# Prompt attention in pairs of key/value heads: one block, plain transposes, the scaling on GpSimd

## What is computed

```
ck = compress_blocks(kv[:, :, :2], cmp_w)
p_c = masked_softmax(jnp.einsum('bqhgd,bnhd->bqhgn', qg, ck[:, :, 0]), mask_c)
o_cmp = jnp.einsum('bqhgn,bnhd->bqhgd', p_c, ck[:, :, 1])
...
o = g[..., 0:1] * o_cmp + g[..., 1:2] * o_slc + g[..., 2:3] * o_win
```

## Time and profile before

| | us |
|---|---|
| median of 3 runs | 2150.6 |
| lowest, highest | 2147.47, 2154.2 |
| profiled execution, first to last instruction (its span) | 2151.5 |
| busy: TensorE | 1927.7 (90%) |
| busy: VectorE | 1031.1 (48%) |
| busy: ScalarE | 669.4 (31%) |
| busy: GpSimd | 240.4 (11%) |

### The profile page before, as it was taken

The page is one execution under the profiler, slowest core; times in us unless marked ns, Lnnn a source line. Parts: engine busy times, 40 slices in busy tenths (PEclk is TensorE's granted clock), DMA queues, the critical chain, the costliest instruction groups (busy, mean ns, idle before and its releaser), DMA issues. The chain is left out here.

```text
span 2151.5 us, 31716 instructions
## 1 busy us (share of the span) xinstructions
PE 1927.7 (90%) x13190; PEld 1745.7 (81%) x13190; DVE 1031.1 (48%) x1718; ACT 669.4 (31%) x1288; POOL 240.4 (11%) x388
## 2 busy tenths in 40 slices
PE   6997998896999999996998969788779699999996
PEld 6996666595999999986798958555478699999995
DVE  5563753235666662226463233336652566665223
ACT  2642442224333332115353220111121533333112
POOL 0010000000222220000100010123000122221000
PEclk9996999798999999998999977668789899999998
DMA  4201620011222222213112230100221222222221
GB/s 170 69 32 46 218 83 2 21 60 59 89 79 83 85 77 81 81 35 101 60 60 79 79 121 1 44 1 0 89 81 37 88 79 86 82 80 83 81 76 58
DMA packets 50321, 152.42 MB, mean 71 GB/s; under 512 B 7282, under 2 KB 16946, under 8 KB 49410
## 3 DMA queue, kind: packets, MB, share of 16 engines
q1 hardware_dynamic: 50178, 150.40, 21.6%
HBM read 138.12 MB, written 16.39 MB: 72 GB/s over the span
## 5 line engine op out<-in xcount | busy, mean ns | idle before, releaser
L686 PE MATMUL ps<-x_high,w_high 128*128 128x288 f32 x2288 | 689.8, 301 | 73.9 <-DVE x_low L708 72.6
L687 PE MATMUL ps<-x_low,w_high 128*128 128x288 f32 x2288 | 681.9, 298 | 0.0
L688 PE MATMUL ps<-x_high,w_low 128*128 128x288 f32 x2288 | 679.5, 297 | 0.0
L686 PEld LDWEIGHTS ps<-x_high,w_high 128*128 128x128 f32 x2288 | 435.6, 190 | 81.7 <-issue 51.0
L665 DVE TENSOR_TENSOR w_low<-w_raw,w_high 128x1024 fp32r<-128x1024 f32 (+1 forms) x215 | 253.5, 1182 | 441.0 <-ACT w_high L660 440.9
L688 PEld LDWEIGHTS ps<-x_high,w_low 128*128 128x128 f32 x2288 | 437.6, 191 | 0.0
L687 PEld LDWEIGHTS ps<-x_low,w_high 128*128 128x128 f32 x2288 | 436.6, 191 | 0.3
L660 ACT ACTIVATE w_high<-w_raw 128x1024 fp32r<-128x1024 f32 (+1 forms) x215 | 221.4, 1032 | 529.6 <-PE ps L688 458.9
L686 PE MATMUL ps<-g_high,w_high 128*128 128x288 f32 x704 | 211.1, 300 | 1.7 <-ACT ub L771 1.7
L687 PE MATMUL ps<-g_low,w_high 128*128 128x288 f32 x704 | 207.7, 295 | 0.0
L688 PE MATMUL ps<-g_high,w_low 128*128 128x288 f32 x704 | 206.9, 294 | 0.0
(11 more groups left out here) (399 smaller groups left out, 2485.6 us busy)
## 6 DMA issues: line engine op xcount, KB each, us to landing
w_raw<-in_w_up SPq DMA_DIRECT2D x88, 512.0 KB, 3.6
w_raw<-in_w_odd SPq DMA_DIRECT2D x36, 512.0 KB, 3.3
w_raw<-in_w_down SPq DMA_DIRECT2D x32, 512.0 KB, 3.6
w_raw<-in_w_even SPq DMA_DIRECT2D x19, 512.0 KB, 3.4
ptok<-in_cache_tok SPq DMA_DIRECT2D x32, 192.0 KB, 2.4
w_raw<-in_w_down SPq DMA_DIRECT2D x16, 384.0 KB, 3.1
w_raw<-in_w_mix SPq DMA_DIRECT2D x16, 384.0 KB, 3.1
w_raw<-in_w_mix SPq DMA_DIRECT2D x8, 512.0 KB, 3.6
```

The costliest lines, as they stand in the source:

```text
L686: pe.matmul(out, self.high[:, s, k, :], high(k0 + k)[:, cols], start=first, stop=False)
L687: pe.matmul(out, self.high[:, s, k, :], low(k0 + k)[:, cols], start=False, stop=False)
L688: mm = pe.matmul(out, self.low[:, s, k, :], high(k0 + k)[:, cols], start=False, stop=last)
```

## The change

Both blocks become one. The loop runs over 32 pairs: the two groups `h` of the same tile, branch and head together. A pair's scores go to two neighbouring PSUM banks, its weighing alternates between the groups product by product. VectorE masks and takes the negated maximum of both groups in one instruction each. It multiplies the reciprocals of the two sums by the gates, and GpSimd scales the probabilities with them in place (`spread`). The turn is then a plain transpose with the identity. ScalarE copies the turned probabilities of group 0, VectorE those of group 1. In step i TensorE takes the scores of pair i, the weighing of pair i-3 and the turn of pair i-2. The compressed branch's scores alternate between the groups; after VectorE has centred them, the rest of that branch runs between the first pairs, with the two multiplications of its probabilities on GpSimd, and its products with the values close each query tile's sums instead of opening them. SyncE's list is the same, in the one block. In the cut diff a line of "..." stands for what is left out.

```diff
+    pairs = [(qt, br, j) for qt in range(4) for br in range(2) for j in range(4)]
+    N = len(pairs)
+    SLOTS = 3
+    S, TURNED, OUT = (0, 2), (4, 5), (6, 7)
...
-            with nc.Block() as block:
...
-        S, TURNED, OUT = (0, 1, 2), (3, 4), (6, 7)
...
+        probs, pT = sb("probs", [P, SLOTS, 2, 512]), sb("pT", [P, 2, 2, 512])
+        nmx, sums = sb("nmx", [P, SLOTS, 2]), sb("sums", [P, SLOTS, 2])
...
+        def keys(p):
+
+            return P * (pairs[p][0] + 1)
...
-                def turn(u):
-
-                    pe.wait_ge(diag_done, u + 1)
-                    if u >= 2:
-                        pe.wait_ge(turned_in, u - 1)
-                    for k in range(units[u][0] + 1):
-                        mm = pe.matmul(net.ps[:, TURNED[u % 2], P * k:P * k + P], probs[:, u % 3, P * k:P * k + P], diag[:, u % 3, :], start=True, stop=True)
-                    mm.then_inc(turned, 1)
...
+                def scores(p):
+
+                    qt, br, j = pairs[p]
+                    if p >= 2:
+                        pe.wait_ge(exped, 2 * (p - 1))
+                    for h in range(2):
+                        mm = pe.matmul(net.ps[:, S[p % 2] + h, 0:keys(p)], qT[64 * h:64 * h + 64, j, P * qt:P * qt + P],
+                                       kT[64 * h:64 * h + 64, br, 0:keys(p)], start=True, stop=True)
+                    mm.then_inc(scored, 1)
+
+                def turn(p):
+
+                    for h in range(2):
+                        pe.wait_ge(normed, 2 * p + h + 1)
+                        if p == 0:
+                            pe.wait_ge(c_taken, h + 1)
+                        else:
+                            pe.wait_ge((kept0, kept1)[h], p)
+                        for k in range(pairs[p][0] + 1):
+                            mm = pe.transpose(net.ps[:, TURNED[h], P * k:P * k + P], probs[:, p % SLOTS, h, P * k:P * k + P], net.ident[:])
+                        mm.then_inc(turned, 1)
+
+                def weigh(p):
+
+                    qt, br, j = pairs[p]
+                    bank, first = OUT[qt % 2], p % 8 == 0
+                    if first and qt >= 2:
+                        pe.wait_ge(out_kept, qt - 1)
+                    if p == 8:
+                        pe.wait_ge(c_kept, 2)
+                    pe.wait_ge(kept0, p + 1)
+                    pe.wait_ge(kept1, p + 1)
                     for k in range(qt + 1):
-                        mm = pe.matmul(net.ps[64 * h:64 * h + 64, bank, P * j:P * j + P], kv[:, k, v0:v0 + 64], pT[:, u % 2, P * k:P * k + P],
-                                       start=False, stop=(br == 1 and k == qt), skip_group_check=True)
-                    mm.then_inc(summed, 1)
-
-                for i in range(N + 4):
+                        for h in range(2):
+                            v0 = (384 if br == 0 else 640) + 64 * h
+                            mm = pe.matmul(net.ps[64 * h:64 * h + 64, bank, P * j:P * j + P], kv[:, k, v0:v0 + 64], pT[:, p % 2, h, P * k:P * k + P],
+                                           start=(first and k == 0), stop=False, skip_group_check=True)
+                    mm.then_inc(weigh_done, 1)
+                    if p % 8 == 7:
+                        pe.wait_ge(c_kept, 2)
+                        for jj in range(4):
+                            for h in range(2):
+                                mm = pe.matmul(net.ps[64 * h:64 * h + 64, bank, P * jj:P * jj + P], cvd[:, h, jj, :], pTc[:, h, qt, :],
+                                               start=False, stop=(jj == 3), skip_group_check=True)
+                        mm.then_inc(weighed, 1)
+
+                for tt in range(4):
...
+                pe.wait_ge(kept, 1)
+                for qt in range(4):
+                    for j in range(4):
+                        for h in range(2):
+                            mm = pe.matmul(net.ps[:, 4 + h, P * qt + 32 * j:P * qt + 32 * j + 32],
+                                           qT[64 * h:64 * h + 64, j, P * qt:P * qt + P], ckT[64 * h:64 * h + 64, :], start=True, stop=True)
+                mm.then_inc(c_scored, 1)
+                for i in range(N + 3):
                     if i < N:
                         scores(i)
+                    if i >= 3:
+                        weigh(i - 3)
                     if 2 <= i < N + 2:
                         turn(i - 2)
-                    if i >= 4:
-                        weigh(i - 4)
+                    if i in (4, 5):
+                        h = i - 4
+                        pe.wait_ge(c_probs, h + 1)
+                        if h:
+                            pe.wait_ge(c_kept, 1)
+                        for qt in range(4):
+                            mm = pe.transpose(net.ps[:, 7, P * qt:P * qt + P], sc[:, h, qt].rearrange("p j n -> p (j n)"), net.ident[:])
+                        mm.then_inc(c_turned, 1)
...
             @block.scalar
             def _(act):
+                def keep(p):
+
+                    act.wait_ge(turned, 2 * p + 1)
+                    if p >= 2:
+                        act.wait_ge(weigh_done, p - 1)
+                    act.activation(pT[:, p % 2, 0, 0:keys(p)], net.ps[:, TURNED[0], 0:keys(p)], ACT.Copy).then_inc(kept0, 1)
+
+                for h in range(2):
+                    act.wait_ge(c_centred, h + 1)
+                    act.activation(sc[:, h], sc[:, h], ACT.Exp).then_inc(c_exped, 1)
                 for i in range(N + 5):
...
                     if i < N:
...
-                            act.wait_ge(turned, i - 2)
-                        act.activation(probs[:, i % 3, 0:n], net.ps[:, S[i % 3], 0:n], ACT.Exp, bias=nmx[:, i % 3:i % 3 + 1],
...
+                        if i >= SLOTS:
+                            act.wait_ge(turned, 2 * (i - SLOTS) + 2)
+                        for h in range(2):
+                            act.activation(probs[:, s, h, 0:keys(i)], net.ps[:, S[i % 2] + h, 0:keys(i)], ACT.Exp, bias=nmx[:, s, h:h + 1],
+                                           accum_out=sums[:, s, h:h + 1]).then_inc(exped, 1)
+                    if 1 <= i < N + 1:
+                        keep(i - 1)
+                    if i in (3, 4):
+                        act.wait_ge(c_turned, i - 2)
+                        act.activation(pTc[:, i - 3], split_free(net.bank(7), t=4, n=P), ACT.Copy).then_inc(c_kept, 1)
+                    if i >= 11 and i % 8 == 3:
+                        qt = i // 8 - 1
+                        act.wait_ge(weighed, qt + 1)
...
+            @block.gpsimd
+            def _(pool):
+                def spread(p):
+
+                    n, s = keys(p), p % SLOTS
+                    pool.wait_ge(shares, p + 1)
+                    for h in range(2):
+                        pool.tensor_scalar(probs[:, s, h, 0:n], probs[:, s, h, 0:n], sums[:, s, h:h + 1], 1.0, ALU.mult, ALU.mult).then_inc(normed, 1)
+
+                keep = split_free(c["cmp_01"], t=4, n=32)[:, :, None, :].broadcast_to([P, 4, 4, 32])
+                for h in range(2):
+                    s16 = sc[:, h].rearrange("p t j n -> p (t j) n")
+                    spread(h)
+                    pool.wait_ge(c_scaled, h + 1)
+                    pool.tensor_tensor(sc[:, h], sc[:, h], keep, ALU.mult).then_inc(c_order, 1)
+                    pool.wait_ge(c_order, h + 1)
+                    pool.tensor_tensor(s16, s16, sm[:, h].rearrange("p t j -> p (t j)")[:, :, None].broadcast_to([P, 16, 32]), ALU.mult).then_inc(c_probs, 1)
+                for p in range(2, N):
+                    spread(p)
 
...
-                for i in range(N + 2):
...
-                        r = sums[:, u % 3:u % 3 + 1]
-                        dve.wait_ge(exped, u + 1)
-                        if u >= 3:
-                            dve.wait_ge(turned, u - 2)
...
+                def centre(h):
+
+                    s16 = sc[:, h].rearrange("p t j n -> p (t j) n")
+                    m16 = mx[:, 16 * h:16 * h + 16]
+                    link(dve.tensor_reduce(m16, s16, AX, ALU.max))
+                    dve.tensor_tensor(s16, s16, m16[:, :, None].broadcast_to([P, 16, 32]), ALU.subtract).then_inc(c_centred, 1)
+
+                def share(h):
+
+                    s16, r16 = sc[:, h].rearrange("p t j n -> p (t j) n"), sm[:, h].rearrange("p t j -> p (t j)")
+                    dve.wait_ge(c_exped, h + 1)
+                    link(dve.tensor_reduce(r16, s16, AX, ALU.add))
+                    link(dve.reciprocal(r16, r16))
+                    dve.tensor_tensor(sm[:, h], sm[:, h], g5[:, 0:4, h, :, 0], ALU.mult).then_inc(c_scaled, 1)
+
+                dve.wait_ge(blocks, 1)
+                dve.tensor_copy(ckT[:], net.ps[:, 7, 0:32])
...
+                dve.wait_ge(c_scored, 1)
+                for h in range(2):
+                    dve.tensor_tensor(sc[:, h], split_free(net.bank(4 + h), t=4, j=4, n=32), neg, ALU.add).then_inc(c_taken, 1)
+                dve.wait_ge(c_taken, 2)
+                for h in range(2):
+                    centre(h)
```

(27 more changed lines are left out.)

124 lines of the change are left out of this document (20 added, 104 removed).

## The result

The changed kernel took 2072.9 to 2095.2 us in four runs, median 2084.2, beside 2147.5 to 2154.2 (median 2152.2) of the kernel before: ratio 0.965, 95% interval 0.959 to 0.972. The prediction was 2084, range 2066 to 2106. The profiled execution took 2086.2 us, its span is 2084.5 (before: 2151.5), so between the two profiles lie 67.0 us.

The account below looks back on a forecast made before the run. TensorE bounds the loop, a chain of dependent steps the compressed block. Pairs 74.6, filling 5.5, branch products 3.4, clock 4.3 and end 7.0 sum to 94.8 against 149.4 us; with 12.1 in front, 66.7 gained: 2084 us, range 2066 to 2106.

Parts of the forecast that it names:

- Heads side by side: Loop on TensorE: full overlap, so a pair's scores and weighing each cost what one head's cost; 3.16 us at four blocks.
- The rival's price: Not side by side: scores and weighing in series, 2124 us; one of the two alone, 2102 or 2105; chance 0.07.
- Plain transposes: Turn on TensorE: a transpose has one pass, not two, so a pair's turn is eight passes at 512 keys.
- VectorE, GpSimd, ScalarE hidden: Long pairs: VectorE 2.82 us, GpSimd scaling 1.4 and ScalarE about 2.1, under TensorE's 3.16.
- the rule at its worst: VectorE and GpSimd blocking in SBUF, one 0.69 us wait per pair: 2106 us; part of the GpSimd rival, chance 0.03.
- Front: Compressed block before the loop: alternating scores 6.7 us instead of 13.0, first mask at 187.2, 12.1 us gained.
- Filling and end: Loop's start and finish: 5.5 us for filling with the compressed branch's work, 7.0 for the last pair beyond its slot.
- Clock: Loop's start: first ten pairs at 1.2 GHz, costing 4.3 us; sample attention starts with a warm TensorE as today.
- The rival of the low clock: TensorE stays at 1.2 GHz: 2130 us; 2091 if it rises after pair 16, 2106 after 24; 16 or more cold, chance 0.07.
- Loads: SyncE's loads for the sample attention: last issue at 234 us, hidden before the sample attention starts near 282.

Follow-up runs that it names:

- the scores apart: Changed kernel with an earlier pair's weighing placed between the scores of the two heads; median 2133.7 us, ratio 0.9842 to the kernel before.
- the turn by products: Changed kernel with the turn as an fp32 product with the identity instead of a transpose; median 2097.3 us, ratio 0.9713 to the kernel before.
- the earlier start: Changed kernel, scores of pairs 0 and 1 ahead of the compressed scores: 2081.2 us, 0.963; second version, compressed scores split over more banks: 2076.4 us, 0.9616.
- the woven kernel before: Kernel before with only the compressed scores alternating between the two heads; median 2163.2 us, ratio 0.9996 to the kernel before.

## Why the prediction was right, point by point

**Heads side by side: right.** Full overlap was taken, and four score passes in 1.13 us and sixteen weighing passes in 1.09 show it, at 3.10 us a pair for the predicted 3.16 (2.45 for 2.52, 1.93 for 2.02). The rival's price was mis-sized in both of its halves: one alone was to add 18 to 21 us. The weighing head after head adds 5.8, since some of its passes still overlap; the scores apart add some 42 at equal mean clock, since the later scores also make the weighing wait for VectorE.

**Plain transposes: right.** Eight passes in 1.09 us; taking them back costs 18.2 us.

**VectorE, GpSimd, ScalarE hidden: right.** GpSimd's 0.69 at 512 elements came from the row of the same operation and is what it takes (1.36 for two). Doubling GpSimd's work costs 4.9 us and not 28, so the slack that the prediction described was there. What the prediction called the rule at its worst, 2106, did not come. VectorE's products with two inputs in SBUF were held up at the loop's start: the 128x16 one took 1.17 us beside a GpSimd product, where the other of its kind took 0.18, and one of the 128x2 kind 0.96 instead of 0.16; both end within 0.05 us of the GpSimd product that was running. This agrees with the Trainium skill, "SBUF — State Buffer" (Who interferes with whom). In the steady loop the product comes when GpSimd is idle, as was argued, and takes 0.16; in all, some 2 us.

**Front: right.** 12.3 us earlier to the first mask (block's start taken as zero) for the predicted 12.1, and the 7.04 us of the compressed scores for 6.7.

**Filling and end: both off, in opposite directions.** From the first mask to pair 8, 18.2 us are eight pairs at the 1.97 us that pairs 6 and 7 took at the low clock, and 2.4: the filling was 2.4, not 5.5, probably because the branch's work on VectorE and GpSimd mostly lay beside the slower TensorE, which no run tested by itself. The end was 12.65, less 3.10 for the pair and 0.9 for the branch's products: 8.6 instead of 7.0.

**Clock: the step that failed.** "I assume the first ten pairs at 1.2 GHz" took one number where there is a range: twelve pairs in one profile, seven in the other. And "the stage behind is unchanged and starts with a warm TensorE as today" missed 3.5 us of the profiled result, since its clock fell for 37 us instead of 27. So the agreement of 66.7 predicted and 67.0 measured between the profiles is partly luck. At a favourable clock the attention gains 75 us (178.1 to 103.0). The prediction's terms held 8 us too much against that (94.8 for 86.7), and the first profile of the change lost 8.3 to the clock, 4.8 in the loop and 3.5 in the sample attention: the two cancel.

**The rival of the low clock** has the right price as far as it was seen: six more cold pairs, 19 us of loop, were to cost 6.8, which is 0.36 us per us, and the two profiles give 4.8 for 13.4, the same. The causes that it named are not borne out. Idle time of TensorE is not needed: with the scores apart the clock stayed at 0.50 with TensorE busy 57.7 of 58 us. The Trainium skill, "TensorE: Matmul & The Clock Gate" (Part 4), holds that transposes don't count as TensorE being busy in the same way; by that rule the change would tend to stay cold, and the turn by products less so. No run here bears it out: with transposes as a third of a pair's phases the clock rose after 31 and 45 us (31 to 42 in the other variants that keep the two heads' scores together), with products after 32, and with products and the scores apart only after 97. But a loop that stays at 0.50 for 86 to 97 us did occur, in two variants that differ from the change in a few lines, and runs of either lie more than 25 us apart. A chance of 0.07 was low for that.

**Loads: right.** SyncE's last load for the sample attention is issued at 233.24 (234 predicted), before it is wanted; the sample attention starts at 279.05 (near 282).

## What to carry to other kernels

Products on two halves of the array overlapped fully here only where they alternate in the program, instruction by instruction; head after head some of the overlap is lost, and with other work between them all of it and more, because the later one delays whoever needs both. A term for the clock needs the granted clock by stretch from more than one execution, and gets a range, not a count of cold pairs: here it moved 8 us of a gain of 67. A change worth less than that, like the earlier start's 4 us, is read from the stage in the trace at equal clock, not from the median.

## What the hardware showed that was not expected

- The granted clock fell to 0.50 between 169.8 and 173.0 in every profile, around the block's start. It rose 31.3 and 44.7 us after the block's first product in two executions of one kernel, and 86 and 97 us after it in the two with scores apart, although TensorE was busy 57.7 of 58 and 68 of 68 us before those rises. In the kernel before, where a head's scores also stand alone, it rose after 38 us in both profiles, so that alone isn't the cause. What brings it back was not found.
- It can fall again in the middle of work: in the woven kernel before at 211.6, with TensorE busy 6.5 of the 7 us ahead of it, and then for 27 us in which TensorE was busy throughout.
- Passes of a later product for the other column half start before those of the earlier one are over, three passes ahead, but not all eight: 16 passes in 1.58 us head after head, 1.09 when alternated.
- Of the same fp32 scaling of 512 elements, VectorE takes 0.48 us and GpSimd 0.69, close enough that the slower engine was the better place.
